# Output waits placed behind the overflow branch, and two row additions put before and after eight final norms

## The reference

```python
x = x + pool_mixer(rms_norm(x, norm_mix), pool_w, pool_scale)
x = x + hier_moe(rms_norm(x, norm_ffn), ...)   # 32 experts, top-2, F = 512
return rms_norm(x, norm_final)                 # x * rsqrt(mean(x*x) + eps) * w
```

## Time and profile before

| | before |
|---|---|
| median of 3 runs | 702.45 us (702.41 to 703.47) |
| profiled execution, its own time | 702.48 us |
| span of the profile | 700.7 us |
| outside the span | 1.78 us |
| mean granted clock of PE | 0.981 |

### The profile page before, as it was taken

One profiled execution on the slowest core, in us unless ns is written; L12 is line 12 of the kernel. 1 busy time (PEld: TensorE's weight loads), 2 busy tenths in 40 slices (PEclk: granted clock), 3 DMA queues, 4 the chain that ended last, 5 costly groups with the idle time before them and its releaser, 6 DMA issues.

```text
span 700.7 us, 10723 instructions
## 1 busy us (share of the span) xinstructions
PE 661.0 (94%) x3652; PEld 557.7 (80%) x3652; DVE 607.9 (87%) x467; ACT 527.8 (75%) x441; POOL 246.9 (35%) x195
## 2 busy tenths in 40 slices
PE   7799979999999999999999999999999999999950
PEld 5799968888888888888888888888888888888740
DVE  6787798889999999999999999999999999999893
ACT  6697626878777777777777777788777777777890
POOL 3000023144444445444444544444444544412201
PEclk9999999999999999999999999999999999999985
DMA  8998768999999999999999999999999999990473
GB/s 314 412 410 250 282 267 317 361 358 387 377 381 386 376 377 380 386 376 382 364 392 386 378 383 388 379 385 375 394 387 378 383 387 377 386 357 12 140 283 133
DMA packets 45002, 242.21 MB, mean 346 GB/s; under 512 B 9646, under 2 KB 10806, under 8 KB 20402
## 3 DMA queue, kind: packets, MB, share of 16 engines
q1 hardware_dynamic: 34322, 220.39, 80.2%
q0 software_dynamic: 10656, 21.50, 11.3%
HBM read 229.82 MB, written 29.36 MB: 370 GB/s over the span
## 4 chain that ended last, share of the span: by engine, by line
PE 88%; DVE 6%; ACT 2%; issue 1%; POOL 1%; DMA 0%; ACTq 0%; POOLq 0%; DVEq 0%
PE psum L1417 73%; PE psum L1437 4%; PE psum L1346 3%; PE psum L1448 2%; PE psum L1332 2%; PE psum L1364 2%; DVE raw L1251 1%; PE psum L1355 1%; DVE w_lo L1004 1%; DVE xs L931 1%; DVE pw L969 0%; ACT xs L706 0%; DMA out<-raw 0%; PE psum L1406 0%; DVE xg L1259 0%
## 5 line engine op out<-in xcount | busy, mean ns | idle before, releaser
L1004 DVE TENSOR_TENSOR w_lo<-raw,w_hi 128x2048 fp32r<-128x2048 f32 x192 | 436.9, 2291 | 48.1 <-ACT w_hi L744 47.9
L744 ACT ACTIVATE w_hi<-raw 128x2048 fp32r<-128x2048 f32 x192 | 364.2, 1915 | 38.9 <-PE psum L1417 38.9
L1417 PE MATMUL psum<-w_hi,x_hi 128*128 128x512 f32 x512 | 162.6, 399 | 0.4 <-DVE w_lo L1004 0.3
L1417 PE MATMUL psum<-w_lo,x_hi 128*128 128x512 f32 x512 | 158.7, 391 | 0.0
L1417 PE MATMUL psum<-w_hi,x_lo 128*128 128x512 f32 x512 | 158.2, 390 | 0.0
L605 POOL DMA_INDIRECT total<-ysb,dst_now x30 | 56.2, 1873 | 224.0 <-ACT ysb L819 224.0
L1417 PEld LDWEIGHTS psum<-w_hi,x_lo 128*128 128x128 f32 x512 | 96.1, 188 | 21.1
L1417 PEld LDWEIGHTS psum<-w_lo,x_hi 128*128 128x128 f32 x512 | 96.1, 188 | 21.0
L1417 PEld LDWEIGHTS psum<-w_hi,x_hi 128*128 128x128 f32 x512 | 91.3, 188 | 22.1 <-DVE w_lo L1004 5.7
L1417 PE MATMUL psum<-w_hi,h_hi 128*128 128x512 f32 x256 | 82.0, 401 | 0.0
L1417 PE MATMUL psum<-w_lo,h_hi 128*128 128x512 f32 x256 | 79.6, 392 | 0.0
(11 more groups left out here) (147 smaller groups left out, 640.8 us busy)
## 6 DMA issues: line engine op xcount, KB each, us to landing
raw<-in_expert_w_gu SPq DMA_DIRECT2D x128, 1024.0 KB, 8.5
raw<-in_expert_w_down SPq DMA_DIRECT2D x64, 1024.0 KB, 7.4
res<-in_x SPq DMA_DIRECT2D x8, 512.0 KB, 9.1
normed<-nx POOLq DMA_DIRECT2D x8, 512.0 KB, 7.0
total<-res SPq DMA_DIRECT2D x8, 512.0 KB, 7.6
raw<-total SPq DMA_DIRECT2D x8, 512.0 KB, 9.2
out<-raw SPq DMA_DIRECT2D x8, 512.0 KB, 2.7
pw_in<-in_pool_w SPq DMA_DIRECT2D x1, 1024.0 KB, 8.0
```

Of the source, the lines that this page charges most:

```text
L744: nc.scalar.activation(w_hi[:, r, :], raw[q][:], ACT.Copy).then_inc(hi_done, 1)
L1004: V.tensor_tensor(w_lo[q][:], raw[q][:], w_hi[:, r, :].bitcast(f32), ALU.subtract)\
L1417: last = mm(dst[:, n * N:(n + 1) * N], a[:, ch, :], b[:, c * D + n * N:c * D + (n + 1) * N], start=(ch == 0 and a is hi and b is b_hi), st ...
```

## The change

Three edits. On SP the two waits for `out_stored` and `late_stored` go from ahead of `If(n)` to behind it (and, for the case that the branch is taken, into it as well). On POOL the wait for `late_stored` goes into the branch, so that POOL no longer waits for its own scatters when `n` is zero; its wait for `out_stored` ahead of the scatters stays. On DVE `late_add(0)` goes ahead of norm 0 and `late_add(1)` behind norm 7.

```diff
             def finish(turn):
                 ...
-                sp.wait_ge(out_stored, 16 * TILES * (turn + 1))
 
             sp.wait_ge(y_stored, 16 * (E - LATE))
             sp.wait_ge(pair_used, MAIN - RAW + TILES)
             finish(0)
-            sp.wait_ge(late_stored, 16 * LATE)
 
             with sp.If(n):
 
+                sp.wait_ge(out_stored, 16 * TILES)
+                sp.wait_ge(late_stored, 16 * LATE)
                 ...
                 finish(1)
+                sp.wait_ge(out_stored, 2 * 16 * TILES)
+
+            sp.wait_ge(out_stored, 16 * TILES)
+            sp.wait_ge(late_stored, 16 * LATE)
```

```diff
                     .then_inc(late_stored, 16)
-            pool.wait_ge(late_stored, 16 * LATE)
 
             with pool.If(n):
 
-
+                pool.wait_ge(late_stored, 16 * LATE)
                 pool.wait_ge(pair_used, MAIN)
```

```diff
             dve.wait_ge(nfin_in, 16)
             dve.wait_ge(gates_made, 1)
+            late_add(0, Y, MAIN - GU_PAIRS // 2)
             for i in range(TILES):
-                if i == 1:
-                    late_add(0, Y, MAIN - GU_PAIRS // 2)
-                if i == EARLY:
-                    late_add(1, GU, MAIN)
                 final_norm(i, 0)
+            late_add(1, GU, MAIN)
             for k in range(LATE):
                 late_norm(k)
```

More of the change, by code:

```diff
@@ L55, in hybrid_pool_moe @@
     FLIGHT = 4
-    EARLY = 4
     UNROLL = 3
```

## The result

The changed kernel takes 698.30 us (median of 6 runs, 698.22 to 699.84) against 702.54 us for the kernel before (6 runs, 702.37 to 703.47). The ratio is 0.9943, with a 95% interval of 0.9930 to 0.9956. The profiled execution took 698.28 us, and its span is 696.5 us.

The account below looks back on a forecast made before the run. PE bounds the whole span, but POOL's DRAIN sets the end. From the profiled 702.48 us, 1.9 us from DVE's order and 2.4 us from POOL's wait gave 4.3 us less: 698.2 us, 8-in-10 range 697.2 to 700.8.

Parts of the forecast that it names:

- What bounds the end: At the closing barrier: POOL's DRAIN of 6172 ns sets the end, reached only after a wait for its own scatters.
- DVE's order: DVE's norms and late additions: addition 0 in idle time, addition 1 behind norm 7; second scatter ends 1.91 us earlier.
- The writes: Whole-tile writes, now 1.39 us apart: backlog delaying the eighth landing taken as zero, bounds 0 to 0.7 us.
- The wait: POOL's removed wait ahead of its branch: DRAIN's work starts when POOL is free, worth 2.4 us.
- a bet (0.48): POOL's last DRAIN: 6.17 us of work done once from when the engine is free; 698.2 us, chance 0.48.
- The first: Rival at POOL's last DRAIN: waits for the scatters' landing, then takes 6.17 us; 700.0 or 700.5 us, chance 0.35.
- The short DRAIN: Rival at POOL's last DRAIN: long before only through the wait, so SP's landing sets the end; 693.9 us, chance 0.06.
- The double one: Rival at POOL's last DRAIN: finds transfers open and goes round twice, 12.34 us; 704.4 us, chance 0.04.
- The backlog of the writes: Part of the no-gain rival: backed-up writes take back the order's gain, with the first rival's second form; 701.5 to 703, chance 0.07.
- shorter code would move the loop: Part of the no-gain rival: moved instructions shift the 600 us loop by one or two us; 701.5 to 703, chance 0.07.

Follow-up runs that it names:

- the order alone: Kernel before with only DVE's edit (late_add(0) ahead of norm 0, late_add(1) behind norm 7), both waits ahead of the branch: 701.43 us, ratio 0.9971.
- twelve DMAs more: Changed kernel, no early DRAIN, POOL issuing twelve 64-byte copies behind its late gathers and waiting for them; DRAIN ended at 703.9, span grew by 7.6 us.
- POOL's wait alone: Kernel before with only POOL's wait for late_stored moved into the branch: 699.88 us, ratio 0.9954.
- the slow copy: Changed kernel plus a DRAIN behind POOL's late gathers and a 4 MB copy of total behind the scatters; copy landed at 707.7, DRAIN ended at 707.8.
- ahead of step 28: Changed kernel with a DRAIN ahead of POOL's step 28 and the late_stored wait back ahead of the branch; last DRAIN took 769 ns behind eight DMAs.
- the early-drain kernel: Changed kernel with one more POOL DRAIN right behind the gathers of the late rows: 694.75 us, ratio 0.9882.
- SP's waits ahead: Changed kernel plus a DRAIN behind POOL's late gathers, with SP's two waits back ahead of its branch: 695.40 us, ratio 0.9887.
- addition 0 behind norm 0: Changed kernel with addition 0 back behind norm 0, addition 1 still behind norm 7: 698.88 us, ratio 0.9951.

## Why the prediction was right, and where not

**What bounds the end.** Right. Every run in which POOL's last DRAIN had 74 or more DMAs to work off ended with that DRAIN, 3.6 us or more after SP was done.

**DVE's order.** Right in each of DVE's steps. Addition 0 was forecast at 671.45 and came at 671.34; reciprocal 0 at 672.64 and 672.53; reciprocal 7 at 682.38 and 682.28; the end of the last late norm at 688.18 and 687.98. The first scatter ran 1.19 us instead of the 1.01 that I took from before, so that the second ended at 690.17 and not at 690.03, although DVE was 0.2 us ahead of my sum. The term is 1.77 us instead of 1.91. The gap ahead of the last late norm was 0.15 us instead of some 0.3.

One statement of the prediction does not hold: that the write's landing would keep the scatters as late as the last late norm does. In the changed kernel the first scatter ended 0.89 us behind the end of DVE's last scaling (688.87 against 687.98), and with the order alone, where the write landed faster and the first scatter began earlier, it ended 0.89 us behind it again (689.86 against 688.97). Against the last weight split the second scatter stands at the same place in both (669.13 and 689.18, 670.12 and 690.16). So the last late norm of DVE set the end there, and not the landing. The number came out all the same, as the two differed by little.

**The writes.** The eighth landed 3.04 us behind its release (683.79), against 2.95 before, and none of the eight took longer. No backlog built up.

**The wait.** The size was right, 2.4 us (4.2 less 1.77), and so was the rule that the work begins when POOL is free. The DRAIN lasted 7.21 us instead of 6.9, as POOL came to it at 689.1 and not at 689.35 and the second scatter ended 0.14 us later. The reason for the 6.17 us stood open in the prediction, so that the number rested on a bet (0.48) that the traces could not decide. The runs give another reason than either rule of the Trainium skill that I weighed. The load of code at a first call (the Trainium skill, "GPSIMD Engine Reference", instruction dispatch) would be paid once; but a DRAIN of 274 ns and one of 769 ns, both behind an earlier one and told apart by the number of DMAs, and 7.1 us with twelve DMAs more, don't fit it. The about 12 ns of a frame's DRAIN (the Trainium skill, "VectorE: DVE Perf Modes", the DRAIN you can't avoid) agree with the 13 ns of SP in the changed kernel, but with none of POOL's: the shortest at the closing barrier was 274 ns, and the 693.9 us of that rule would need a short one here. What fits the DRAINs of 274, 769 and 6172 ns behind an idle engine, and the 7.1 us with twelve more, is about 82 ns for each DMA that POOL has issued since its last DRAIN.

**The rivals.** The first, a DRAIN that waits for the landing and then takes its 6.17 us, fell (the end would have come at 700.0 us, and with POOL's wait alone the DRAIN ended at 697.9 and not at 700.0), but half of its premise is true: the slow copy shows that a DRAIN waits for the landing. I had put the two one behind the other; they run beside each other, and the end is the later of the two. Here the work is 6.13 us and the landing comes 1.9 us behind the second scatter, so that the work decides. The short DRAIN is what the kernel gets once its backlog is gone, and the time of 694.2 to 695.5 is near the 693.9 that stood for it. The double one, over 11 us, fell with the DRAIN of 7.21 us. The backlog of the writes was tried with the order alone, and fell. That shorter code would move the loop was not tried by itself; one addition of the loop came up to 2.6 us apart in the traces (602.45 to 605.06), each of another kernel, and the kernel before scattered by 2.5 us with its code unchanged.

## What to carry to other kernels

Look behind the last transfer: POOL's DRAIN at the barrier can be long if POOL has issued many DMAs (here 6.2 us behind 74), and a DRAIN placed where POOL waits anyway can take that off the end. The place must be one where no gather stands close behind it: ahead of step 28 it cost 1.4 us. Take waits that only guard the end of the program from POOL and give them to an engine that has nothing to do at the barrier, behind its branch. In a row of equal operations that feed transfers, put the foreign ones into the idle time ahead of the first, or behind the last.

## What the runs showed of the hardware

- A DRAIN of POOL with the engine idle and all landed took 274 ns with 2 DMAs since the last one, 769 with 8, 6172 with 74: about 82 ns a DMA. Twelve DMAs of 64 bytes added 1.0 us, what the slope says, so it is not by bytes.
- It also waits for POOL's transfers in flight, and works the backlog off meanwhile: with two or three DMAs since the last one it ended 0.1 to 0.2 us behind the landing in three traces (the early-drain kernel, the slow copy, SP's waits ahead), and with 74 it ended 6.13 us behind the second scatter in the changed kernel, whose landing came 1.9 us behind it. SP's transfers did not hold it: the DRAIN ahead of step 28 ended at 615.1 with the queues at 406 GB/s in 613 to 615.
- Behind fresh gathers or additions, with the queues busy, a DRAIN took longer: that of the early-drain kernel lasted until 673.05, 10.1 us from POOL's being free (662.91) for 72 DMAs, where the slope says 6.0. What moved there were mostly the loads of `total` (396 GB/s in 663 to 671) and no longer weights: from 630 to 640 nothing had moved at all. That ahead of step 28, beside weight loads, took 10.5 us for 66, where the slope says 5.6. In all six traces with such a DRAIN it ended 2.8 to 3.1 us behind the landing of POOL's last transfer (670.04 in the early-drain kernel, 612.3 ahead of step 28), so waiting alone doesn't explain it. Why, was not tried.
- POOL's first scatter takes longer the more it overlaps DVE's last scaling (1.28 us): 1.01 us with no overlap, 1.19 and 1.20 with 0.3 us of it (changed kernel, addition 0 behind norm 0), 1.60 and 1.58 with 0.7 us (order alone, SP's waits ahead). In each of these four traces it ends 0.89 us behind the end of the scaling, as if it stood still until then. That DVE's scaling holds it is argued from these distances; no run was made for it.
